# Two fused transformer layers in fp32: indexer weights moving instead of stationary, latents turned in blocks, unit and mix transfers rescheduled

## The chip, the cores and the metric

One NeuronCore of a Trainium2 chip runs the whole program. The metric is device time in microseconds (us); three runs of the kernel before are shown, and one more execution was profiled.

## What is computed

x is 256 tokens of 2048 features, fp32. Two layers follow one another.

Layer 1: h = rmsnorm(x), z = h @ w_in (2048 x 5200). The columns of z are: a pooling input, q, k, v (8 heads of 128), 16 index queries of 64, one index key of 64 and 16 index weights (the last 80 columns: "kw"). The index scores select 64 keys for each query; attention runs over them; the outputs of attention and of a pooling mixer go through w_out; then a gated feed-forward with a convolution over three tokens (w_up, w_down).

Layer 2, cut to what the change touches:

```
q_a, k_a, v_a, c_q, c_kv, k_r, gates = split(rmsnorm(h) @ w_in_2)
y_a = moba_attention(rope(q_a), rope(k_a), v_a)
qh  = rmsnorm(c_q)  @ w_uq_2          # c_q: 256 x 512, "cq"
kv  = rmsnorm(c_kv) @ w_ukv_2         # c_kv: 256 x 256, "ckv"
y_b = mla_attention(qh, kv, rope(k_r))
mixed = sigmoid(g_a) * (y_a @ w_branch_a_2) + sigmoid(g_b) * (y_b @ w_branch_b_2)
h = h + mixed @ w_out_2
h = h + (silu(hn @ w_gate_2) * (hn @ w_up_2)) @ w_down_2     # hn = rmsnorm(h)
```

## The kernel before, in words

**Products.** Every fp32 operand is split in two fp32r halves, hi and lo, and a product is hi*hi + hi*lo + lo*hi. Weights arrive in chunks of 256 rows (two k-tiles) by 512 columns into w_raw, a ring of 4 slots. ScalarE copies a chunk to w_hi (`split`, L1081), VectorE subtracts to w_lo (L1447), and TensorE (`columns`, L747 to L757) runs 2 k-tiles x 2 token tiles x 3 products = 12 matmuls with a 128x128 block of the activation stationary and 512 weight columns moving. The matmuls of one group (512 output columns) add up in one of two pairs of PSUM banks, acc[0] and acc[1].

**Order.** `plan` (L55) lists the groups with their first chunk and puts every other step at a chunk number n, in the table `at`. TensorE runs the steps of n behind chunk n. ScalarE and VectorE run them behind their split of chunk n + 3 (LEAD). SP runs them behind the load of chunk n + 7 (L513, `chunk.now - RING - LEAD - 1`); a load of chunk c waits until w_lo of chunk c - 4 is done. Each engine works through its list in order, so a step that waits holds up the splits or loads behind it. In a group whose last chunk is b - 1, the steps "at b" are the ones that follow it.

**kw.** The group of 80 columns (L128) has two chunks of eight k-tiles. `kw_columns` (L791) holds the 80 weight columns stationary and moves the 256 tokens: 16 k-tiles x 3 = 48 matmuls, the result being 80 x 256, turned. ScalarE copies it to stage (`on_copy_kw`, L1133), TensorE turns it back (`turn_kw`, L852, two transposes), VectorE scales it (`on_evac_kw`, L1453). `turn_ki` (L861) turns the doubled index key.

**Turning by blocks.** A tile is turned in two parts: VectorE transposes 32x32 blocks (L1601, L1621), then 16 SBUF-to-SBUF transfers of 32 partitions each put the blocks in their places (`move_block`, L378, its dma_start is L382; `move_unit`, L544; `move_p`, L413, whose dma_start is L419). A "unit" is one of the 12 groups of index queries, q, k, qa, ka, qn, qr that are turned so. All 16 transfers of a unit are on SP, in four steps of four. For p (attention weights) the first eight are on SP and the last eight on ScalarE's queue (`move_p_rest`). The latents cq and ckv are turned by TensorE instead (`on_turn_lat`, L986: 8 and 4 transposes of 128x128 against ident, L745), and split from PSUM by ScalarE and VectorE (`on_split_lat`, L1231, L1586).

**Mixed groups.** For n = 0 to 3 there is a group of w_branch_a_2 and one of w_branch_b_2, four chunks each. Behind the second, at b, VectorE forms the mixed columns (`on_mix_b`, L1695: two multiplications at L1699, two additions at L1702, two block transposes at L1601) and signals mix_blocks. Then 16 transfers (stage to halves) follow: for n < 3 all on SP, four each at b, b+1, b+2, b+3; for n = 3 ten on SP at b and six on ScalarE at b+1 (`move_mix_rest`). ScalarE (`on_split_mix`, L1236, L1239) waits for all 16 and makes the hi half of m_hl, VectorE (L1591, L1595) the lo half, at b+7, for n = 3 at b+3. b of one n is 8 chunks before b of the next. w_out_2 starts at b of n = 3; its chunks 4, 5, 6 and 7 wait for the lo halves of n = 2 and n = 3, two quarters each (L1048 on, `need`).

Of the kernel before, what the change touches and what calls it, by code (L numbers as in the profile page):

```python
# [6 lines left out]
F32 = mybir.dt.float32  # L7
F32R = mybir.dt.float32r
I32 = mybir.dt.int32
ALU = mybir.AluOpType  # L10
# [44 lines left out]
def plan():  # L55
# [15 lines left out]
    def copy_out(n, kind, *dest):  # L71
# [20 lines left out]
        for b in range(4):  # L92
            put(n + lead + later + b, "move", u, g, b)
# [35 lines left out]
    put(b, "copy_kw", len(groups) - 1); put(b + 1, "turn_kw", len(groups) - 1); put(b + 1, "evac_kw")  # L129
    put(b + 3, "turn_ki"); put(b + 4, "copy_ki")  # L130
# [60 lines left out]
    for n in range(4):  # L191
# [42 lines left out]
def two_layer_kernel(nc, a, out):  # L234
# [6 lines left out]
    with ctx:  # L241
# [107 lines left out]
        kw_turned, kw_scaled = sem("kw_turned"), sem("kw_scaled")  # L349
# [15 lines left out]
        p_blocks, p_moved = sem("p_blocks"), sem("p_moved")  # L365
        mix_blocks, mix_moved = sem("mix_blocks"), sem("mix_moved")
# [23 lines left out]

        def shares(part):

            return range(SP_SHARE) if part is None else range(4 * part, 4 * part + 4)
# [52 lines left out]
        def unit_there(u):  # L446

            return unit_moved[u % 4], 256 * (u // 4 + 1)

# [33 lines left out]
        def _(sp):  # L483
# [12 lines left out]
            def load(name, col, width, c):  # L496
# [15 lines left out]
                if not chunk.per:  # L512
                    if 20 <= chunk.now < 25:  # L513
                        load_constant(chunk.now - 20)
                    for step_, *args in at.get(chunk.now - RING - LEAD - 1, []):
                        if step_ == "move_x":
                            move_x(sp, args[0], shares(args[1]))
                        elif step_ == "move_mix":
                            move_mix(sp, args[0], shares(args[1]))
# [4 lines left out]
                        elif step_ == "move":  # L524
                            move_unit(*args)
# [18 lines left out]
            def move_unit(u, g, b):  # L544

                if b == 0:
                    sp.wait_ge(unit_blocks, u + 1)
                    if units[u][0:2] == ("qa", 1):
                        sp.wait_ge(scores_full, 6)
                    elif units[u][0:2] == ("ka", 1):  # L550
                        sp.wait_ge(*unit_there(u - 2))
                to, from_ = unit_target(u, g), unit_source(u)
                for a_ in range(4):
                    if units[u][0] in ("k1", "ka"):
# [1364 lines left out]
```

## Time and profile before

| | |
|---|---|
| median of three runs | 2373.63 us |
| lowest, highest | 2372.42, 2373.67 us |
| the profiled execution | 2370.55 us, span 2368.8 us from first to last instruction |
| instructions | 29833, of them 10552 matmuls |
| mean granted TensorE clock | 0.999 |
| weights and other reads from HBM | 448.12 MB, 190 GB/s over the span |

Busy time overlaps between engines. A matmul's own duration (390 ns for 512 columns) is longer than the distance between two matmuls, because they are pipelined: costs on TensorE are read from the starts. "PEld" is the load of the stationary operand, which runs beside the matmul before it. "SPq" and "ACTq" are the issues of transfers by SP and ScalarE.

### The profile page before, as it was taken

The numbers are of one execution on the slowest core, as the hardware profiler recorded it, in microseconds if no ns is written. First come the engines' busy times: TensorE is split into PE (matmuls) and PEld (weight loads), VectorE is DVE, ScalarE is ACT, GpSimd is POOL, SyncE is SP. The second block draws the span as 40 slices with busy tenths as digits, with TensorE's granted clock in tenths as the row PEclk, the third lists the DMA queues.
The fourth block names the chain that finished last, engine by engine and source line by source line (L and its number), as shares of the span: only waits on it lengthen the run. The fifth ranks groups of instructions, "written<-read, shape, count | busy, mean of one in ns | idle before, by whom it ended". The sixth has DMA issues, their size and how long they took to land.

```text
span 2368.8 us, 29833 instructions
## 1 busy us (share of the span) xinstructions
PE 2354.6 (99%) x10552; PEld 1949.5 (82%) x10552; DVE 1399.9 (59%) x1586; ACT 1186.1 (50%) x1465; POOL 59.4 (3%) x94
## 2 busy tenths in 40 slices
PE   9999999999999999999999999999999999999998
PEld 7788888888888888888888888878888888888887
DVE  6786465676776765555565554766555555554544
ACT  6445455666666544445455554544544444444443
POOL 0000000000000000001130000000000000000000
PEclk9999999999999999999999999999999999999999
DMA  9776477788787766666787666666777777767664
GB/s 304 195 216 192 153 225 209 215 227 220 202 226 219 206 219 201 201 203 195 210 215 209 181 175 197 200 202 208 230 204 200 209 203 204 209 199 220 194 195 153
DMA packets 490442, 488.24 MB, mean 206 GB/s; under 512 B 248304, under 2 KB 275568, under 8 KB 490224
## 3 DMA queue, kind: packets, MB, share of 16 engines
q1 hardware_dynamic: 467888, 482.85, 69.5%
q10 hardware_dynamic: 22464, 4.20, 0.9%
q8 instruction: 56, 0.92, 0.2%
q14 instruction: 34, 0.28, 0.0%
HBM read 448.12 MB, written 2.10 MB: 190 GB/s over the span
## 4 chain that ended last, share of the span: by engine, by line
PE 96%; SPq 1%; DVE 1%; DMA 1%; ACT 0%; issue 0%; POOLq 0%; POOL 0%; DVEq 0%; ACTq 0%
PE acc L754 31%; PE acc L756 31%; PE acc L755 31%; SPq L382 1%; PE pair_banks L923 1%; DMA w_raw<-in_w_branch_a 1%; DVE w_lo L1447 0%; PE bank L942 0%; ACT w_hi L1081 0%; DMA w_raw<-in_w_in 0%; PE pair_banks L972 0%; PE pair_banks L895 0%; PE acc L780 0%; PE acc L784 0%; PE acc L787 0%
## 5 line engine op out<-in xcount | busy, mean ns | idle before, releaser
L1447 DVE TENSOR_TENSOR w_lo<-w_raw,w_hi 128x1024 fp32r<-128x1024 f32 (+1 forms) x842 | 1024.1, 1220 | 934.8 <-ACT w_hi L1081 933.2
L1081 ACT ACTIVATE w_hi<-w_raw 128x1024 fp32r<-128x1024 f32 (+1 forms) x842 | 886.0, 1055 | 1077.1 <-PE acc L756 980.9
L754 PE MATMUL acc<-w_hi,xT 128*128 128x512 f32 (+1 forms) x2208 | 861.4, 390 | 0.0
L756 PE MATMUL acc<-w_hi,xT 128*128 128x512 f32 (+1 forms) x2208 | 856.8, 388 | 0.0
L755 PE MATMUL acc<-w_lo,xT 128*128 128x512 f32 (+1 forms) x2208 | 856.7, 388 | 0.0
L754 PEld LDWEIGHTS acc<-w_hi,xT 128*128 128x128 f32 x2208 | 414.5, 188 | 87.1 <-issue 2.7
L756 PEld LDWEIGHTS acc<-w_hi,xT 128*128 128x128 f32 x2208 | 414.5, 188 | 85.4
L755 PEld LDWEIGHTS acc<-w_lo,xT 128*128 128x128 f32 x2208 | 414.6, 188 | 83.8
L754 PE MATMUL acc<-w_hi,f_hi 128*128 128x512 f32 x688 | 267.6, 389 | 0.0
L755 PE MATMUL acc<-w_lo,f_hi 128*128 128x512 f32 x688 | 267.6, 389 | 0.0
L756 PE MATMUL acc<-w_hi,f_lo 128*128 128x512 f32 x688 | 267.6, 389 | 0.0
L755 PEld LDWEIGHTS acc<-w_lo,f_hi 128*128 128x128 f32 x688 | 129.2, 188 | 27.0
L754 PEld LDWEIGHTS acc<-w_hi,f_hi 128*128 128x128 f32 x688 | 129.2, 188 | 26.7
L756 PEld LDWEIGHTS acc<-w_hi,f_lo 128*128 128x128 f32 x688 | 129.2, 188 | 26.7
L754 PE MATMUL acc<-w_hi,y_hi 128*128 128x512 f32 x256 | 100.0, 391 | 0.0
L756 PE MATMUL acc<-w_hi,y_lo 128*128 128x512 f32 x256 | 99.6, 389 | 0.0
L755 PE MATMUL acc<-w_lo,y_hi 128*128 128x512 f32 x256 | 99.6, 389 | 0.0
L755 PEld LDWEIGHTS acc<-w_lo,y_hi 128*128 128x128 f32 x256 | 48.1, 188 | 10.0
L754 PEld LDWEIGHTS acc<-w_hi,y_hi 128*128 128x128 f32 x256 | 48.1, 188 | 9.9
L756 PEld LDWEIGHTS acc<-w_hi,y_lo 128*128 128x128 f32 x256 | 48.1, 188 | 9.9
L754 PE MATMUL acc<-w_hi,m_hl 128*128 128x512 f32 x128 | 49.9, 390 | 3.8 <-DVE w_lo L1447 3.8
L755 PE MATMUL acc<-w_lo,m_hl 128*128 128x512 f32 x128 | 49.8, 389 | 0.0
(211 smaller groups left out, 1217.4 us busy)
## 6 DMA issues: line engine op xcount, KB each, us to landing
w_raw<-in_w_up SPq DMA_DIRECT2D x264, 512.0 KB, 4.2
w_raw<-in_w_in SPq DMA_DIRECT2D x198, 512.0 KB, 4.3
w_raw<-in_w_down SPq DMA_DIRECT2D x176, 512.0 KB, 4.5
w_raw<-in_w_gate SPq DMA_DIRECT2D x88, 512.0 KB, 3.7
w_raw<-in_w_out SPq DMA_DIRECT2D x64, 512.0 KB, 4.3
w_raw<-in_w_branch_a SPq DMA_DIRECT2D x16, 512.0 KB, 4.5
w_raw<-in_w_branch_b SPq DMA_DIRECT2D x16, 512.0 KB, 4.4
halves<-stage SPq DMA_DIRECT2D x234, 32.0 KB, 2.7
```

Of the source, the lines that this page charges most:

```text
L382: return queue.dma_start(dst, src)
L754: pe.matmul(o, l, w_hi[:, slot, k, 0:width], start=start, stop=False)
L755: pe.matmul(o, l, w_lo[:, slot, k, 0:width], start=False, stop=False)
L756: last = pe.matmul(o, m, w_hi[:, slot, k, 0:width], start=False, stop=stop)
L923: last = pe.matmul(pair_banks[:, j, blk * P:blk * P + nk], q[:, blk * P:(blk + 1) * P], k[:, 0:nk], start=alone or blk == 0, stop=alone, s ...
L1081: act.activation(in_slot(w_hi, slot, width), in_slot(w_raw, slot, width), ACT.Copy).then_inc(w_split_hi, 1)
L1447: dve.tensor_tensor(in_slot(w_lo, slot, width), in_slot(w_raw, slot, width), in_slot(w_hi, slot, width).bitcast(F32), ALU.subtract).then_i ...
```

## The change

Half of every unit's transfers (blocks 2 and 3) are issued by ScalarE, in steps of their own. The kw group holds the tokens stationary (128x128) and moves the 80 weight columns, hi and lo; the result has the tokens on partitions, and VectorE scales it from acc; the two TensorE transposes and ScalarE's copies go. The transfers of mixed groups 0 to 2 come in three steps of 6, 6 and 4 at b+2 to b+4 instead of four at b to b+3; those of group 3 at b+2 on both queues (before b and b+1) and its split at b+5 (before b+3). The latents are turned by VectorE in blocks, with 16 transfers each on SP at b+2 to b+5, and are split at b+13 (before b+2). The diff, cut to its core:

```diff
         for b in range(4):
-            put(n + lead + later + b, "move", u, g, b)
+            put(n + lead + later + b, "move" if b < 2 else "move_rest", u, g, b)
         if name in ("k1", "ka"):
...
-    put(b, "copy_kw", len(groups) - 1); put(b + 1, "turn_kw", len(groups) - 1); put(b + 1, "evac_kw")
-    put(b + 3, "turn_ki"); put(b + 4, "copy_ki")
+    put(b, "evac_kw", len(groups) - 1)
+    put(b + 2, "turn_ki", len(groups) - 1); put(b + 3, "copy_ki")
...
-    put(b + 1, "turn_lat", "cq", len(groups) - 1)
-    put(b + 2, "split_lat", "cq"); put(b + 2, "lat_rstd", "cq")
+    put(b + 1, "lat_blocks", "cq", len(groups) - 1)
+    for part in range(4):
+        put(b + 2 + part, "move_lat", "cq", part)
+    put(b + 13, "split_lat", "cq"); put(b + 2, "lat_rstd", "cq")
...
-    put(b + 1, "turn_lat", "ckv", len(groups) - 1)
-    put(b + 2, "split_lat", "ckv"); put(b + 2, "lat_rstd", "ckv"); put(b + 1, "rope", "kr", len(groups) - 1)
+    put(b + 1, "lat_blocks", "ckv", len(groups) - 1)
+    for part in range(4):
+        put(b + 2 + part, "move_lat", "ckv", part)
+    put(b + 13, "split_lat", "ckv"); put(b + 2, "lat_rstd", "ckv"); put(b + 1, "rope", "kr", len(groups) - 1)
...
-        for part in range(4) if n < 3 else (None,):
-            put(b + (part or 0), "move_mix", n, part)
+        for part in range(3) if n < 3 else (None,):
+            put(b + 2 + (part or 0), "move_mix", n, part)
         if n == 3:
-            put(b + 1, "move_mix_rest", n)
-        put(b + (7 if n < 3 else 3), "split_mix", n)
+            put(b + 2, "move_mix_rest", n)
+        put(b + (7 if n < 3 else 5), "split_mix", n)
...
+        def thirds(part):
+
+            return range(SP_SHARE) if part is None else range(6 * part, min(6 * part + 6, 16))
...
+        def latents(kind):
+
+            if kind == "cq":
+                return 0, 4, over_y[0][:], over_y[4][:], cqT, G_CQ
+            return 1, 2, over_y[1][:, 0:CW], over_y[1][:, CW:2 * CW], ckvT, G_CKV
+
+        def turned_latent(kind, q):
+
+            _, nq, _, moved, _, _ = latents(kind)
+            return moved.rearrange("p (n q k) -> p n q k", n=2 * 4, q=nq)[:, :, q]
 
         def p_source(which, pair):
 
...
         def unit_there(u):
 
             return unit_moved[u % 4], 256 * (u // 4 + 1)
+
+        def move_unit(queue, u, g, b):
+
+            if b % 2 == 0:
+                queue.wait_ge(unit_blocks, u + 1)
+                if units[u][0:2] == ("qa", 1):
+                    queue.wait_ge(scores_full, 6)
+                elif units[u][0:2] == ("ka", 1):
+                    queue.wait_ge(*unit_there(u - 2))
+            to, from_ = unit_target(u, g), unit_source(u)
+            for a_ in range(4):
+                if units[u][0] in ("k1", "ka"):
+                    move = move_block(queue, to, from_, b, a_)
+                else:
+                    move = queue.dma_start(to[32 * b:32 * (b + 1)].rearrange("p (n a k) -> p n a k", n=8, a=4)[:, :, a_],
+                                        from_[32 * a_:32 * (a_ + 1)].rearrange("p (n b k) -> p n b k", n=8, b=4)[:, :, b])
+                move.then_inc(unit_moved[u % 4], 16)
...
-                            move_mix(sp, args[0], shares(args[1]))
+                            move_mix(sp, args[0], thirds(args[1]))
+                        elif step_ == "move_lat":
+                            move_lat(*args)
...
+            def move_lat(kind, b):
+
+                k, _, blocks_, moved, _, _ = latents(kind)
+                sp.wait_ge(lat_blocks, k + 1)
                 for a_ in range(4):
-                    if units[u][0] in ("k1", "ka"):
-                        move = move_block(sp, to, from_, b, a_)
-                    else:
-                        move = sp.dma_start(to[32 * b:32 * (b + 1)].rearrange("p (n a k) -> p n a k", n=8, a=4)[:, :, a_],
-                                            from_[32 * a_:32 * (a_ + 1)].rearrange("p (n b k) -> p n b k", n=8, b=4)[:, :, b])
-                    move.then_inc(unit_moved[u % 4], 16)
+                    move_block(sp, moved, blocks_, b, a_).then_inc(lat_moved[k], 16)
...
-                    h, l, o = hi[:, k * KW:(k + 1) * KW], lo[:, k * KW:(k + 1) * KW], acc[g][0][0:KW, 0:S]
-                    pe.matmul(o, h, xT_hi[:, kt], start=kt == 0, stop=False)
-                    pe.matmul(o, h, xT_lo[:, kt], start=False, stop=False)
-                    last = pe.matmul(o, l, xT_hi[:, kt], start=False, stop=kt == KT - 1)
+                    h, l = hi[:, k * KW:(k + 1) * KW], lo[:, k * KW:(k + 1) * KW]
+                    for t in range(NT):
+                        o, rows = acc[g][t][:, 0:KW], slice(t * P, (t + 1) * P)
+                        pe.matmul(o, xT_hi[:, kt, rows], h, start=kt == 0, stop=False)
+                        pe.matmul(o, xT_hi[:, kt, rows], l, start=False, stop=False)
+                        last = pe.matmul(o, xT_lo[:, kt, rows], h, start=False, stop=kt == KT - 1)
...
-            def turn_kw(g):
-
+            def turn_ki(g):
                 wait_bank(0)
                 pe.wait_ge(acc_taken[g % 2], 2 * (g // 2 + 1))
-                for t in range(NT):
-                    last = turn(0, t * KW, stage[0:KW, g % 2, 0, t * P:(t + 1) * P], KW)
-                last.then_inc(kw_turned, 1)
-                free[0] = (kw_scaled, NT)
-
-            def turn_ki():
...
-            def on_turn_stage(g, banks, wait):
-                pe.wait_ge(*wait)
-                for b in banks:
-                    wait_bank(b)
-                    four(b, lambda cc, t: stage[:, g % 2, t, (2 * b + cc) * P:(2 * b + cc + 1) * P], split_full, 1)
-                    splits.now += 1
-                    free[b] = (split_lo, splits.now)
-
-            def on_turn_lat(kind, g):
-                on_turn_stage(g, range(2 if kind == "cq" else 1), (acc_taken[g % 2], 2 * (g // 2 + 1)))
-                lats.append(splits.now)
...
-                    need = {0: (split_lo, lats[0])}
+                    need = {0: (lat_low, 1)}
                 elif name == "w_ukv_2" and col == 0:
-                    need = {0: (split_lo, lats[1])}
+                    need = {0: (lat_low, 2)}
...
-            def on_copy_kw(g):
-                finished(g)
-                stage_free(g)
-                for t in range(NT):
-                    act.activation(stage[0:KW, g % 2, 0, t * P:(t + 1) * P], acc[g % 2][0][0:KW, t * P:(t + 1) * P],
-                                   ACT.Copy).then_inc(acc_taken[g % 2], 1)
...
+            def on_move_rest(u, g, b):
+                move_unit(act, u, g, b)
...
-                o, gain = (cqT, G_CQ) if kind == "cq" else (ckvT, G_CKV)
-                for b in range(2 if kind == "cq" else 1):
-                    high([o[:, 0, 2 * b], o[:, 0, 2 * b + 1]], b, gain + 2 * b)
+                k, nq, _, _, o, gain = latents(kind)
+                act.wait_ge(lat_moved[k], 256)
+                for q in range(nq):
+                    last = act.activation(o[:, 0, q].rearrange("p (n k) -> p n k", n=2 * 4), turned_latent(kind, q), ACT.Copy,
+                                          scale=cols[:, gain + q:gain + q + 1])
+                last.then_inc(lat_high, 1)
...
-            def on_evac_kw():
-
-                dve.wait_ge(kw_turned, 1)
+            def on_evac_kw(g):
+
+                finished(g)
                 dve.wait_ge(rstd_ready, 1)
                 for t in range(NT):
-                    r, key = rstd[:, t:t + 1], T[0][:, t * KW:t * KW + IDX_DIM]
-                    dve.tensor_scalar(widx[:, t], T[0][:, t * KW + IDX_DIM:(t + 1) * KW], r, 2.0 ** -5, ALU.mult, ALU.mult)
+                    r, key = rstd[:, t:t + 1], acc[g % 2][t][:, 0:IDX_DIM]
+                    dve.tensor_scalar(widx[:, t], acc[g % 2][t][:, IDX_DIM:KW], r, 2.0 ** -5, ALU.mult, ALU.mult)
                     dve.tensor_scalar(kdup[:, t, 0:64], key, r, None, ALU.mult)
-                    dve.tensor_scalar(kdup[:, t, 64:128], key, r, None, ALU.mult).then_inc(kw_scaled, 1)
+                    dve.tensor_scalar(kdup[:, t, 64:128], key, r, None, ALU.mult).then_inc(acc_taken[g % 2], 1)
 
             def on_headsq(name, g):
...
+            def on_lat_blocks(kind, g):
+                _, nq, blocks_, _, _, _ = latents(kind)
+                dve.wait_ge(acc_taken[g % 2], 2 * (g // 2 + 1))
+                for t in range(NT):
+                    last = dve.transpose(blocks_.rearrange("p (t b q k) -> p t q b k", t=NT, b=4, q=nq)[:, t],
+                                         stage[:, g % 2, t, 0:nq * P])
+                last.then_inc(lat_blocks, 1)
+
             def on_split_lat(kind):
-                o, gain = (cqT, G_CQ) if kind == "cq" else (ckvT, G_CKV)
-                for b in range(2 if kind == "cq" else 1):
-                    low([o[:, 1, 2 * b], o[:, 1, 2 * b + 1]], [o[:, 0, 2 * b], o[:, 0, 2 * b + 1]], b, gain + 2 * b)
+                k, nq, _, _, o, gain = latents(kind)
+                dve.wait_ge(lat_high, k + 1)
+                for q in range(nq):
+                    lo_, hi_ = (o[:, n, q].rearrange("p (n k) -> p n k", n=2 * 4) for n in (1, 0))
+                    last = dve.scalar_tensor_tensor(lo_, turned_latent(kind, q), cols[:, gain + q:gain + q + 1],
+                                                    hi_.bitcast(F32), ALU.mult, ALU.subtract)
+                last.then_inc(lat_low, 1)
```

## Rows read from the trace of the kernel before

**Rows 1.** The page, busy time of each engine: us, share of the span, instructions.
```profile
PE 2354.6 (99%) x10552; PEld 1949.5 (82%) x10552; DVE 1399.9 (59%) x1586; ACT 1186.1 (50%) x1465; POOL 59.4 (3%) x94
```

**Rows 2.** Waits: engine, line, waited for; us in total, times, longest.
```profile
ACT w_hi L1081 <- PE acc L756: 980.9, 658, 8.1
...
PE acc L754 <- DVE w_lo L1447: 3.8, 2, 2.5
```

**Rows 3.** Timeline of TensorE in w_out_2: start us, us, what, [idle before].
```profile
1551.69 0.39 PE L754 MATMUL acc<-w_hi,m_hl 128*128 128x512 f32 x1
...
1562.35 0.39 PE L756 MATMUL acc<-w_hi,m_hl 128*128 128x512 f32 x1
...
1564.02 0.47 PE L754 MATMUL acc<-w_hi,m_hl 128*128 128x512 f32 x1 [1.29 <-DVE w_lo L1447]
...
1569.50 0.47 PE L754 MATMUL acc<-w_hi,m_hl 128*128 128x512 f32 x1 [2.48 <-DVE w_lo L1447]
```

**Rows 4.** The kw group: window (busy us, instructions by engine, clock, DMA) and timeline.
```profile
50.40:55.98 5.58, 5.58 (x49) 5.58 (x48) 2.66 (x3) 3.28 (x4) 0.00 (x0) 1.00 0.89 251
...
50.40 0.15 PEld L799 LDWEIGHTS acc<-xT,w_hi 128*80 128x80 f32 x1
...
50.52 0.28 PE L799 MATMUL acc<-xT,w_hi 128*80 128x256 f32 x1
```

**Rows 5.** Timeline of the weight loads behind the kw transposes.
```profile
61.54 0.19 PEld L754 LDWEIGHTS acc<-w_hi,xT 128*128 128x128 f32 x1
...
61.65 0.19 PEld L755 LDWEIGHTS acc<-w_lo,xT 128*128 128x128 f32 x1
```

**Rows 6.** Timeline of TensorE around the kw and the cq transposes.
```profile
61.23 0.39 PE L756 MATMUL acc<-w_hi,xT 128*128 128x512 f32 x1
...
61.56 0.48 PE L754 MATMUL acc<-w_hi,xT 128*128 128x512 f32 x1
...
61.88 0.40 PE L755 MATMUL acc<-w_lo,xT 128*128 128x512 f32 x1
...
1092.40 0.31 PE L754 MATMUL acc<-w_hi,xT 128*128 128x320 f32 x1
...
1092.69 0.31 PE L756 MATMUL acc<-w_hi,xT 128*128 128x320 f32 x1
...
1093.86 0.31 PE L755 MATMUL acc<-w_lo,xT 128*128 128x320 f32 x1
```

**Rows 7.** Timeline of ScalarE and its queue, transfers of p.
```profile
1210.29 1.06 ACT L1081 ACTIVATE w_hi<-w_raw 128x1024 fp32r<-128x1024 f32 x1 [1.92 <-DMA w_raw<-in_w_in]
...
1210.30 2.62 ACTq L419 DMA_DIRECT2D halves<-over_y  x4
```

**Rows 8.** Timeline of VectorE in the mixing stage, first and last group.
```profile
1491.55 1.30 DVE L1601 STREAM_TRANSPOSE stage<-stage 128x512 f32<-128x512 f32 x2
...
1492.78 2.32 DVE L1447 TENSOR_TENSOR w_lo<-w_raw,w_hi 128x1024 fp32r<-128x1024 f32 x2
...
1558.82 1.28 DVE L1699 TENSOR_TENSOR gate<-acc,gate 128x512 f32<-128x512 f32 x2
...
1561.46 1.30 DVE L1601 STREAM_TRANSPOSE stage<-stage 128x512 f32<-128x512 f32 x2
```

**Rows 9.** Timeline of SP, ScalarE and VectorE around w_out_2's first group.
```profile
1552.25 7.05 SPq L510 DMA_DIRECT2D w_raw<-in_w_out  x5
...
1556.59 1.06 ACT L1081 ACTIVATE w_hi<-w_raw 128x1024 fp32r<-128x1024 f32 x1 [0.61 <-DMA w_raw<-in_w_out]
...
1562.80 4.13 ACTq L382 DMA_DIRECT2D halves<-stage  x6
...
1570.46 1.34 ACT L1239 ACTIVATE m_hl<-halves 128x256 fp32r<-128x256 f32 x4 [1.42 <-DMA halves<-stage]
...
1570.91 1.43 DVE L1595 TENSOR_TENSOR m_hl<-halves,m_hl 128x256 fp32r<-128x256 f32 x4 [0.42 <-ACT m_hl L1239]
```

**Rows 10.** Transfers of L382 (move_block), 1480 to 1575: from issue to landing.
```profile
DMA to landing us min/median/max: 1.8/2.4/3.8
```

More of the change, by code:

```diff
@@ L348, in two_layer_kernel @@
         fgain_loaded, stored = sem("fgain_loaded"), sem("stored")
-        kw_turned, kw_scaled = sem("kw_turned"), sem("kw_scaled")
         gqk_ready, angles, tables = sem("gqk_ready"), sem("angles"), sem("tables")
@@ L365, in two_layer_kernel @@
         p_blocks, p_moved = sem("p_blocks"), sem("p_moved")
+        lat_blocks, lat_high, lat_low = sem("lat_blocks"), sem("lat_high"), sem("lat_low")
+        lat_moved = [sem("cq_moved"), sem("ckv_moved")]
         mix_blocks, mix_moved = sem("mix_blocks"), sem("mix_moved")
@@ L524, in load @@
                         elif step_ == "move":
-                            move_unit(*args)
+                            move_unit(sp, *args)
                         elif step_ == "move_p":
@@ L542, in load_constant @@
                                  allow_slow_non_contiguous=True).then_inc(const_loaded, 16)
[L544 to L552, printed above, removed]
-                for a_ in range(4):
-                    if units[u][0] in ("k1", "ka"):
-                        move = move_block(sp, to, from_, b, a_)
-                    else:
-                        move = sp.dma_start(to[32 * b:32 * (b + 1)].rearrange("p (n a k) -> p n a k", n=8, a=4)[:, :, a_],
-                                            from_[32 * a_:32 * (a_ + 1)].rearrange("p (n b k) -> p n b k", n=8, b=4)[:, :, b])
-                    move.then_inc(unit_moved[u % 4], 16)
+            def move_lat(kind, b):
+                k, _, blocks_, moved, _, _ = latents(kind)
+                sp.wait_ge(lat_blocks, k + 1)
+                for a_ in range(4):
+                    move_block(sp, moved, blocks_, b, a_).then_inc(lat_moved[k], 16)
             def pair(j, wa, ca, wb, cb):
@@ L731, in _ @@
             chunk, group, splits, copies = Count(), Count(), Count(), Count()
-            rels, atts, pvs, lats = Count(), Count(), [0], []
+            rels, atts, pvs = Count(), Count(), [0]
             roped_n, turned_any = [0], []
@@ L849, in stream @@
                 group.now += 1
-            def turn_kw(g):
+            def turn_ki(g):
                 wait_bank(0)
                 pe.wait_ge(acc_taken[g % 2], 2 * (g // 2 + 1))
-                for t in range(NT):
-                    last = turn(0, t * KW, stage[0:KW, g % 2, 0, t * P:(t + 1) * P], KW)
-                last.then_inc(kw_turned, 1)
-                free[0] = (kw_scaled, NT)
-            def turn_ki():
-                wait_bank(0)
                 turn(0, 0, kdup[:, 0])
@@ L1004, in on_turn_kn @@
                 free[0] = (copy_done, copies.now)
-            mine = {"turn_kw": turn_kw, "turn_ki": turn_ki, "turn_copy": turn_copy, "rel": on_rel, "scores": on_scores,
+            mine = {"turn_ki": turn_ki, "turn_copy": turn_copy, "rel": on_rel, "scores": on_scores,
                     "pv": on_pv, "pool_d": on_pool_d, "pool_y": on_pool_y,
-                    "turn_lat": on_turn_lat,
                     "turn_kr": on_turn_kr, "turn_kn": on_turn_kn}
@@ L1280, in on_sigmoid @@
                 act.activation(v, v, ACT.Sigmoid).then_inc(gates_open, 1)
-            mine = {"evac": on_evac, "copy_kw": on_copy_kw, "copy_ki": on_copy_ki, "copy2": on_copy2, "copy_k": on_copy_k, "relu": on_relu, "exp": on_exp,
-                    "copy_d": on_copy_d, "move_p_rest": on_move_p_rest, "copy_kr": on_copy_kr, "copy_kn": on_copy_kn,
+            mine = {"evac": on_evac, "copy_ki": on_copy_ki, "copy2": on_copy2, "copy_k": on_copy_k, "relu": on_relu, "exp": on_exp,
+                    "copy_d": on_copy_d, "move_p_rest": on_move_p_rest, "move_rest": on_move_rest, "copy_kr": on_copy_kr, "copy_kn": on_copy_kn,
                     "split_y": on_split_y, "split_x": on_split_x, "move_x_rest": on_move_x_rest, "move_mix_rest": on_move_mix_rest, "split_pool": on_split_pool,
@@ L1709, in _ @@
                     "select": on_select, "mask": on_mask, "norm": on_norm, "split_y": on_split_y, "split_x": on_split_x,
-                    "split_pool": on_split_pool, "split_lat": on_split_lat, "split_mix": on_split_mix, "res": on_res,
+                    "split_pool": on_split_pool, "lat_blocks": on_lat_blocks, "split_lat": on_split_lat, "split_mix": on_split_mix, "res": on_res,
                     "rstd": on_rstd, "lat_rstd": on_lat_rstd, "mix_a": on_mix_a, "mix_b": on_mix_b,
```

## The prediction

> **What bounds the kernel now.** I read the page's busy times first: TensorE is busy for 2354.6 of 2368.8 us, VectorE 59%, ScalarE 50% [rows 1]. Then its waits: in the whole middle of the run it waits 3.8 us, all for w_lo, in two pieces [rows 2]. Both lie in the first group of w_out_2, the product of the mixed halves [rows 3]. So time can come only from work taken off TensorE and from that one stall; every other engine matters as far as it makes a new stall. ScalarE's w_hi waits 980.9 us for TensorE to free a slot [rows 2]: the split normally runs as far ahead as the ring lets it, three chunks of 12 x 0.227 = 2.72 us (pitch: 47 steps from 1551.69 to 1562.35, [rows 3]). Of these 8.2 us a split needs 1.06 + 1.23 us, so ScalarE can be about 5.9 us late before TensorE sees it.
>
> **The indexer's 80 columns.** Now 48 matmuls have the weights (80 columns) stationary and 256 columns of xT moving; they fill the window 50.40 to 55.98, 5.6 us, 0.117 us each [rows 4]. After it there are 96, with xT (128 columns) stationary and 80 moving. No row has a moving operand so narrow with fp32r. From below, the array's time by columns: from 256 to 512 moving columns the pitch grows from 0.117 to 0.227 us, 0.43 ns a column, so 80 columns would take 0.117 - 176 x 0.00043 = 0.041 us: 96 x 0.041 = 3.9 us, a gain of 1.7. From above, if the narrow form is taken like plain fp32, the transposes of 128 columns have a pitch of 0.109 us (8 in 0.87 us), and two instructions for each product would give 192 x 0.109 = 20.9 us, +15.3. Between them lies the load of the stationary operand. A load of 80 columns lasts 0.15 us and one of 128 lasts 0.19 [rows 4, 5]: 48 columns more cost 40 ns, 0.83 ns each, so 128 columns stream for about 0.107 us. It can be seen bare where a short transpose stands before it: the load of L754 starts at 61.54 and the next at 61.65, 0.11 us, and that matmul lasts 0.48 instead of 0.39 because it waits [rows 5, 6]. Today 512 moving columns hide it; 80 don't. I take 0.11 us, the row that is nearest in kind: 96 x 0.11 = 10.6 us, **+5.0 us**. The same two loads of one xT block behind one another are not merged: L754 and L755 share their stationary operand today and each has its load.
>
> The Trainium skill, page "TensorE: Matmul & The Clock Gate", speaks on both sides. Its section "Back-to-back issue gap" gives an isolated matmul columns / 2.4 + 2.5 ns, 36 ns for 80: by that alone the group would take 3.4 us, a gain of 2.2. Its section "LDWEIGHTS (loading the stationary operand)" gives columns / 1.2, 107 ns for 128: by that 10.2 us, a loss of 4.7; the trace's 0.11 us speaks for the second.
>
> **Transposes that leave TensorE.** cq: from the start of the matmul before the eight transposes to the second one behind them 1092.69 to 1093.86, less two pitches of 0.147 (1092.40 to 1092.69 are two) = 0.87 us. ckv has four, half: 0.44. kw: 61.23 to 61.88, less 2 x 0.227 = 0.20 [rows 6]. Sum **-1.5 us**. In their place stand two block transposes on VectorE (1.3 us, as L1601) in the place of nothing, 16 transfers for each latent on SP, and the same splits, now 13 chunks behind. w_uq_2 follows cq's group by four groups, w_ukv_2 later still: cost 0. In ckv's group a chunk takes only 12 x 0.147 = 1.8 us, while SP with four transfers and a load needs 3.2, so three loads come up to 4.3 us late; the lead of 5.9 covers that. The kw group's steps lose two ScalarE copies and VectorE reads acc directly: 0, as nobody waits.
>
> **Half of the unit transfers on ScalarE.** 12 units, two steps each of four transfers. Such a step exists, for p: four take 2.6 us on ScalarE's queue and are issued while the w_hi before them runs, both from 1210.3 [rows 7]. Split and step together so take about one chunk of 2.72, and each step costs up to 0.2 us of lead, against 5.9. The densest place is qn, qr and qa beside exp and the transfers of p: two such steps, an exp and an output split within three chunks, some 3 us late. SP gets 96 issues less, but its lateness cost nothing. Both 0; if the lead were gone, each step would cost 2.6 us. The added wait for unit_blocks stands two chunks behind VectorE's step; behind it on ScalarE is the next w_hi, and behind that w_lo and TensorE, so it would cost only with VectorE over two chunks late. SP's wait for lat_blocks holds the weight loads in the same way, and comes a load later than VectorE's step: 0.
>
> **The mixed groups.** Call B(n) the moment when VectorE has turned group n. The first is 1491.55 + 1.30 = 1492.85, the last 1562.76 [rows 8]: three turns of 23.3 us, where TensorE needs only 21.8. So the chain is late by a loop of its own. From B: 16 transfers and three loads on SP until the load of w_out_2's fourth chunk is issued at 1552.25 (13.1), 4.3 to land, w_hi 1.1, w_lo 1.2, the mixing step 1558.82 to 1562.76 (3.9) [rows 8, 9]. The change sends two loads ahead of the transfers, which relieves this, but another branch takes over: ScalarE's split_mix stands before the split of that fourth chunk and waits for all 16 transfers. From B: two w_lo 2.3 [rows 8], load 0.6, 6 transfers 3.8, load 0.6, 6 transfers 3.8, load 0.6, three more pitches 1.9: 13.7; landing 2.4 [rows 10], split_mix 1.3, w_hi 1.1, w_lo 1.2, mixing step 3.9: 23.7 us. The same sum for before gives 22.6 where it measured 23.3, so 23.7 to 24.4. B(3) = 1492.85 + 71.1 = 1563.9, up to 1566.0.
>
> For n = 3 the step itself moves. Now SP and ScalarE start at B; the last transfer is there at 1570.46 and two quarters of w_lo of m_hl are done at about 1571.65, B + 8.9 [rows 9]. TensorE needs them at w_out_2's seventh chunk. After it SP stands behind two loads, which wait for two w_lo: 2.3 + 0.6, nine pitches 5.8, 1.9 to land, 1.2: B + 11.8 = 1575.7 to 1577.8. Without a stall that chunk would start at 1551.69 + 6 x 2.72 = 1568.0; it now starts at 1572.3, a loss of 4.3 in all (waits and exposed loads, [rows 3]). After: 7.7 to 9.8. ScalarE's own six, which now cost TensorE 2.48 us because they hold up a split for 8.1 us [rows 2, 9], no longer matter. Difference +3.4 to +5.5; I take **+4.5 us**. From below: if the loop is gone, B(3) is 1551.7 + 1.1 + 1.2 + 3.9 = 1557.9 and the loss 1.7, a gain of 2.6; at most all 4.3 come back.
>
> **Sum.** +5.0 - 1.5 + 4.5 = +8.0 us. The profiled execution took 2370.55 us (span 2368.8), so 2378.6 for one like it; it lies 3.1 below the median of the runs, 2373.63. For the median: **2381.6 us**.
>
> **Rivals.**
> 1. *Narrow matmuls run at their columns.* The load hides behind its neighbours (the two of one xT block could share it); kw becomes -1.7 instead of +5.0. For it: the array's time is 0.43 ns a column. Against: the bare load. Total +1.3: 2374.9. Not slower. It decides wherever the pitch is under 0.075 us. The Trainium skill's gap formula would be this rival.
> 2. *The loop of the mixed groups opens.* The loads that go first let the mixing step start on time, and the transfers land before anyone waits; the whole stall of 4.3 goes. For it: the fourth load is issued 1 to 2 us earlier. Against: split_mix and the later ten transfers. Total 5.0 - 1.5 - 4.3 = -0.8: 2372.8. Not slower.
> 3. *Both 1 and 2*: -7.5, 2366.1, faster.
> 4. *Narrow fp32r is slower than its load*, 0.15 us (as the 320-column matmul) up to two instructions of 0.109: kw +8.8 to +15.3, total +11.8 to +18.3, 2385.4 to 2391.9.
> 5. *ScalarE's lead is used up* near the exp of the second attention: one or two steps of 2.6 us behind the sum, 2384 to 2387.
>
> **How the numbers follow.** A measurement of this kernel tells 0.2% (4.7 us) from no change. Forecast 0.43 (slower), rival 1 0.16, rival 2 0.16, rival 3 0.06, rival 4 0.13, rival 5 0.06. Slower: 0.43 + 0.13 + 0.06 = 0.62, less 0.03 for a forecast whose mixed part is at its lower bound: 0.59. Faster: 0.06 plus 0.02 for rival 2 with a small kw price: 0.08. Same: 0.33. The range takes in rivals 1 and 2 and most of 4: from 2372.5 to 2388.
>
> **What would show it.** kw: 96 matmuls at a pitch of 0.11 us, a window of 10.6 us, loads back to back (0.04: rival 1; 0.15 and more: rival 4). No transposes of the latents; TensorE's wait list with w_lo or m_hl in w_out_2's fifth and seventh chunk, 8 to 9 us in all, and the last VectorE transpose at about 1566 plus what kw cost before it. ScalarE waiting for halves <- stage in each split_mix shows the new branch; if it doesn't wait, rival 2 is near. If TensorE waits anywhere between 1160 and 1260, rival 5 is at work. The forecast is wrong if the pitch is under 0.075 us or if the mixed groups lose under 3 us.

## The result, and the profile after

The changed kernel takes **2391.05 us** (median of 4 runs, 2388.82 to 2392.87), the kernel before 2373.31 beside it (4 runs): ratio 1.0079, 95% interval 1.0067 to 1.0092, so 17.7 us or 0.8% slower. The prediction said slower, with 2381.6 us (+8.0) and an upper end of 2388.0. The direction holds; of the size, less than half was foreseen, and the median lies 3 us above that upper end.

The profiled execution of the changed kernel took 2392.87 us (span 2391.1), that of before 2370.55 (2368.8): 22.3 us between the two traces, the one at the upper edge of its runs, the other below its. The page's first part answers to [rows 1], the wait list to [rows 2] (us in total, times, longest):

```profile
PE 2371.1 (99%) x10586; PEld 1965.8 (82%) x10586; DVE 1402.9 (59%) x1590; ACT 1185.4 (50%) x1463; POOL 59.1 (2%) x94
```
```profile
PE acc L783 <- DVE m_hl L1617: 4.9, 1, 4.9
PE acc L783 <- DVE w_lo L1457: 3.6, 3, 2.1
PE bank L965 <- DMA halves<-over_y: 2.0, 1, 2.0
...
ACT m_hl L1249 <- DMA halves<-stage: 15.1, 4, 4.3
```

TensorE waits 10.5 us in these three rows where it waited 3.8, so only some 7 of the 22.3 are waits. It is also busy for 16.5 us more, with 34 instructions more and 1.5 us of transposes less. Of that, some 3.5 us are work that was added (the narrow matmuls' 5.0 at full clock, less those transposes). The rest is work that ran slower. Where, the start times of the same matmuls in both traces tell, stage by stage:

```
stretch                                          after - before
up to the kw group                                   +0.6
kw group and the first 8 matmuls behind it          +13.0
latents (cq, ckv)                                    -1.4
one product with v, second attention (1256)          +2.4
branch groups, up to w_out_2                         +1.6
w_out_2 (first half)                                 +6.1
sum                                                  22.3
```

**The kw group.** Windows of TensorE (us, busy us, instructions, granted clock as a share of 2.4 GHz, DMA share, GB/s), then single matmuls and loads from the timelines:

```profile
50.00:54.00 4.00, 4.00 (x33) 1.00 1.00 303
54.00:58.00 4.00, 4.00 (x23) 0.55 0.95 210
58.00:62.00 4.00, 4.00 (x21) 0.50 0.73 167
62.00:66.00 4.00, 4.00 (x20) 0.50 0.57 157
66.00:70.00 4.00, 4.00 (x16) 0.50 0.00 0
70.00:74.00 4.00, 4.00 (x16) 0.81 0.53 139
```
```profile
51.22 0.28 PE L829 MATMUL acc<-w_hi,xT 128*128 128x80 f32 x1
51.33 0.28 PE L830 MATMUL acc<-w_lo,xT 128*128 128x80 f32 x1
...
55.14 0.41 PE L831 MATMUL acc<-w_hi,xT 128*128 128x80 f32 x1
55.35 0.41 PE L829 MATMUL acc<-w_hi,xT 128*128 128x80 f32 x1
...
68.15 0.77 PE L783 MATMUL acc<-w_hi,xT 128*128 128x512 f32 x1
68.72 0.63 PE L784 MATMUL acc<-w_lo,xT 128*128 128x512 f32 x1
69.15 0.63 PE L785 MATMUL acc<-w_hi,xT 128*128 128x512 f32 x1
```
```profile
51.19 0.19 PEld L829 LDWEIGHTS acc<-w_hi,xT 128*128 128x128 f32 x1
51.30 0.19 PEld L830 LDWEIGHTS acc<-w_lo,xT 128*128 128x128 f32 x1
...
55.28 0.33 PEld L829 LDWEIGHTS acc<-w_hi,xT 128*128 128x128 f32 x1
55.50 0.33 PEld L830 LDWEIGHTS acc<-w_lo,xT 128*128 128x128 f32 x1
```

For the first 3.5 us (32 of them, 50.96 to 54.50) the narrow matmuls start 0.11 us apart and so do their loads, as predicted. Then the granted clock falls from its upper level, 2.4 GHz, to its lower, 1.2 GHz, with no idle time on TensorE before it: loads and matmuls are now 0.21 us apart, and stay so until the group ends at 68.15. The group takes 17.2 us against 5.6 [rows 4]. The low clock outlives it: the next 8 wide matmuls have a pitch of 0.43 instead of 0.227 us, another 1.7 us. Less 0.2 for the two transposes that are gone, that makes the +13.0.

**w_out_2.** Timelines of SP's queue, of ScalarE and its queue, of VectorE and of TensorE around the last mixed group; they answer to [rows 3, 8, 9]:

```profile
1570.68 12.19 SPq L547 DMA_DIRECT2D w_raw<-in_w_out  x6
1582.92 6.64 SPq L387 DMA_DIRECT2D halves<-stage  x10
```
```profile
1580.27 3.88 ACTq L387 DMA_DIRECT2D halves<-stage  x6
...
1590.83 1.33 ACT L1249 ACTIVATE m_hl<-halves 128x256 fp32r<-128x256 f32 x4 [3.62 <-DMA halves<-stage]
```
```profile
1578.93 1.31 DVE L1623 STREAM_TRANSPOSE stage<-stage 128x512 f32<-128x512 f32 x2
...
1591.28 1.43 DVE L1617 TENSOR_TENSOR m_hl<-halves,m_hl 128x256 fp32r<-128x256 f32 x4 [2.43 <-ACT m_hl L1249]
```
```profile
1567.93 0.39 PE L783 MATMUL acc<-w_hi,m_hl 128*128 128x512 f32 x1
...
1581.49 0.47 PE L783 MATMUL acc<-w_hi,m_hl 128*128 128x512 f32 x1 [2.05 <-DVE w_lo L1457]
...
1592.09 0.79 PE L783 MATMUL acc<-w_hi,m_hl 128*128 128x512 f32 x1 [4.88 <-DVE m_hl L1617]
1592.68 0.63 PE L784 MATMUL acc<-w_lo,m_hl 128*128 128x512 f32 x1
...
1597.32 0.39 PE L783 MATMUL acc<-w_hi,m_hl 128*128 128x512 f32 x1
```

VectorE has turned the last group at 1580.2; SP reaches its ten transfers only at 1582.9, ScalarE's split waits for them until 1590.8, and the seventh chunk starts at 1592.09 instead of 1567.93 + 6 x 2.72 = 1584.25: 7.8 us lost, the lower end of what was predicted. But behind the wait of 4.9 us the clock is at its lower level too: 12 matmuls from 1592.09 to 1597.32 take 5.2 us instead of 2.7.

### The profile page after: what moved, and what is told of

Its sections match the earlier page's. It is cut to its first block, busy times and chain, and to the rows that moved or that the text cites. A ratio compares the mean times of both kernels' runs of the same rounds, so it can differ in the third digit from the quotient of the medians.

```text
span 2391.1 us, 29934 instructions
## 1 busy us (share of the span) xinstructions
PE 2371.1 (99%) x10586; PEld 1965.8 (82%) x10586; DVE 1402.9 (59%) x1590; ACT 1185.4 (50%) x1463; POOL 59.1 (2%) x94
## 4 chain that ended last, share of the span: by engine, by line
PE 95%; SPq 1%; DVE 1%; DMA 1%; ACT 0%; issue 0%; ACTq 0%; POOLq 0%; POOL 0%; DVEq 0%
PE acc L783 30%; PE acc L784 30%; PE acc L785 30%; SPq L387 1%; PE pair_banks L946 1%; DVE w_lo L1457 0%; DMA halves<-stage 0%; PE bank L965 0%; PE acc L809 0%; PE acc L813 0%; PE acc L816 0%; PE pair_banks L995 0%; DMA halves<-over_y 0%; PE pair_banks L918 0%; PE acc L831 0%
```

## The experiments

Fourteen experiments were run: one part of the change alone, one part undone, and the disputed costs by themselves. "At the scores" is the start of the first matmul into pair_banks from kiT (78.4 us in the trace of before): a shift there is what the kw group and its surroundings cost, free of everything later.

**1. The 80 columns alone** (kw_only):
```diff
-    put(b, "copy_kw", len(groups) - 1); put(b + 1, "turn_kw", len(groups) - 1); put(b + 1, "evac_kw")
-    put(b + 3, "turn_ki"); put(b + 4, "copy_ki")
+    put(b, "evac_kw", len(groups) - 1)
+    put(b + 2, "turn_ki", len(groups) - 1); put(b + 3, "copy_ki")
...
-                    pe.matmul(o, h, xT_hi[:, kt], start=kt == 0, stop=False)
...
+                        pe.matmul(o, xT_hi[:, kt, rows], h, start=kt == 0, stop=False)
...
```


> The kernel before with the indexer's 80 columns moving, nothing else. Theory 1 (narrow matmuls pull the granted clock down to half, inside the group and into the next one): the group starts at a pitch of 0.11 us, the clock then falls to half, and TensorE starts the first relu-scores (into pair_banks, from kiT) 12 to 14 us later than before; the whole run takes +12.5 to +13.5 us in its trace. Rival (the price is the load alone; the clock fell for some other part of the change, such as transfers): clock stays at full, pitch 0.11 us throughout, +4.8 us.

Measured: 2381.23 us against 2371.51, ratio 1.0039 (1.0025 to 1.0053), +9.7; at the scores +12.7. Its windows:
```profile
50.00:54.00 4.00, 4.00 (x35) 0.92 0.96 298
54.00:58.00 4.00, 4.00 (x21) 0.50 0.67 166
```
The clock falls here with none of the other parts present. That is theory 1 up to the scores. Its +12.5 to +13.5 for the whole run is missed, because the rest of the run gave some back: in w_out_2 TensorE waited 1.8 us instead of 3.8, and the span is 10.9 us longer, not 12.7.

**2. The other three parts, each alone** (mix_only, units_only, lat_only): the diff's lines for that part and no others.

> The kernel before with only the mixed groups' transfers and splits moved. Theory 1 (the loss is made in this stage alone, by the transfers of n = 3 standing two loads later and the turns of the mixing loop staying at 24 us): +6 us, with a wait of about 5 us on m_hl at the seventh chunk of w_out_2 and the clock at half after it. Rival (the stage was late only because the units' transfers and the kw group had changed the phase): under +3 us, no fall of the clock there.

> The kernel before with half of each unit's transfers on ScalarE's queue, nothing else. Theory 1 (in the second attention the transfers of p land late because ScalarE's queue carries the unit's, and TensorE waits at one product with v): +2 to +2.5 us, in one wait of about 2 us near 1256. Rival a: 0, and the wait in the changed kernel came from the latents' transfers or the shifted phase. Rival b: the wait is there and the branch stage adds another, +4 us.

> The kernel before with only the latents turned in blocks. Theory 1: the 12 transposes go from TensorE and nothing is late: -1.4 us (0.87 + 0.44 = 1.3 from the rows of before). Rival: the 32 transfers on SP make the loads or the unit transfers behind them late, and the time is the same as before or longer.

Measured against the same 2371.51 us: mix_only 2377.34, ratio 1.0025 (1.0015 to 1.0034), +5.8; units_only 2371.29, ratio 1.0000 (0.9991 to 1.0010); lat_only 2369.24, ratio 0.9993 (0.9983 to 1.0003), -2.3 and in the trace -1.3 between the scores of the first and of the second attention. mix_only has the wait on m_hl (5.6 us) and the low clock behind it: its shift grows by 7.3 us in the stage. The wait at a product with v isn't in units_only. With kw_only the four sum to +13.1, against +17.7 together.

**3. A wide matmul between the narrow ones** (kw_wide_between, kw_wide_sixth). In the first:
```diff
                         pe.matmul(o, xT_hi[:, kt, rows], l, start=False, stop=False)
+                        pe.matmul(T[3][:, 0:CW].rearrange("p (k s) -> p k s", k=2), xT_hi[:, kt, rows], xT_hi[:, 0:2], start=True, stop=True)
                         last = pe.matmul(o, xT_lo[:, kt, rows], h, start=False, stop=kt == KT - 1)
```
In the second the same line (with rows 0 to 127) stands once behind every six.

> As kw_only, with one matmul of 512 moving columns (its product goes to a bank that nobody reads) behind every two narrow ones and ahead of the third: 32 of them, at the 0.227 us of a wide one 7.3 us of added work. Theory 1 (the clock falls because of the run of narrow matmuls with nothing wide among them): granted clock stays at full through the group, 96 x 0.11 + 7.3 = 17.8 us for the group, +12.3 against before, none of it behind the group. Rival (the clock falls there whatever stands between them, for example by the transfers or by the change of bank): it falls as in kw_only, and the group takes 24 us or more.

> As kw_only, with one added matmul of 512 moving columns behind every six narrow ones: 16 of them, 3.6 us of added work. Theory 1a (a wide one in seven is enough to keep the granted clock at full): 96 x 0.11 + 3.6 = 14.2 us for the group, +8.4 against before, so less than kw_only's +12.7 though more is done. Theory 1b (it is too little): the clock falls as in kw_only, later in the group or at the same place, and the cost is +13 to +20.

Measured at the scores: +12.2 and **+8.2** us (forecast 12.3 and 8.4). The clock is whole in both, as these windows show, of kw_wide_between first:
```profile
54.00:56.00 2.00, 2.00 (x16) 1.00 0.83 224
...
66.00:68.00 2.00, 2.00 (x16) 1.00 0.30 49
```
```profile
54.00:58.00 4.00, 4.00 (x33) 1.00 0.81 184
58.00:62.00 4.00, 4.00 (x33) 1.00 0.78 180
```
By medians: 2383.42 (2 runs) against 2371.50, ratio 1.0053 (1.0033 to 1.0073), and 2381.76 (3 runs) against 2371.38, 1.0042 (1.0027 to 1.0057). kw_wide_sixth does 16 matmuls more than kw_only and reaches the scores 4.5 us earlier. The mean granted clock of every execution agrees with the traces: 0.995 or 0.996 in all five of kw_only, 0.998 or 0.999 in these five. The whole run did not become shorter, though: +10.4 by the median against +9.7 for kw_only, with intervals that overlap. Behind the scores kw_only's trace gives back 1.8 us in w_out_2, where that of kw_wide_sixth loses 1.0, with the lower clock behind a wait. So neither the transfers nor the change of bank makes the clock fall there; the unbroken run of narrow matmuls does. Taking the added 3.6 us off, the 96 narrow ones at full clock cost 4.6 more than before: the +5.0 of the prediction, less the transposes of kw.

**4. Two thirds of the loads** (kw_160). xT_hi meets 160 columns of w_hi in one matmul; the product xT_hi x w_lo is left out.
```diff
-                        pe.matmul(o, xT_hi[:, kt, rows], h, start=kt == 0, stop=False)
-                        pe.matmul(o, xT_hi[:, kt, rows], l, start=False, stop=False)
+                        pe.matmul(o[:, 0:2 * KW], xT_hi[:, kt, rows], hi[:, min(k, 6) * KW:(min(k, 6) + 2) * KW], start=kt == 0, stop=False)
```


> As kw_only, but xT_hi meets 160 columns of w_hi in one matmul, in the place of two of 80 against w_hi and w_lo (so the product xT_hi x w_lo is left out and the indexer's keys and weights are off): 64 matmuls, 32 of 160 and 32 of 80 columns. If the load of the stationary operand alone sets the pitch at full clock: 64 x 0.11 = 7.0 us for the group, +1.4 against before. Theory 1a (the clock falls with narrow matmuls also when a third fewer of them are there): the group starts at 0.11 us and the clock falls within it or right behind it, +4 to +7. Theory 1b (the wider moving operands hold the clock): +1.4 and no fall.

Measured at the scores: **+1.0 us** (forecast +1.4), and no fall:
```profile
54.00:56.00 2.00, 2.00 (x20) 1.00 0.84 189
56.00:58.00 2.00, 2.00 (x16) 1.00 0.85 194
```
```profile
56.70 0.32 PE L825 MATMUL acc<-w_hi,xT 128*128 128x160 f32 x1
56.86 0.23 PE L826 MATMUL acc<-w_hi,xT 128*128 128x80 f32 x1
56.92 0.32 PE L825 MATMUL acc<-w_hi,xT 128*128 128x160 f32 x1
57.08 0.24 PE L826 MATMUL acc<-w_hi,xT 128*128 128x80 f32 x1
57.15 0.48 PE L779 MATMUL acc<-w_hi,xT 128*128 128x512 f32 x1
```
A pair of 160 and 80 columns takes 0.22 us, like a pair of 80 and 80: the number of loads sets the time, not the columns. Whole run: 2371.12 against 2371.50 us, ratio 0.9999 (0.9989 to 1.0009), with a mean granted clock of 0.998 to 1.000 in all eight executions. Whether the wider operand keeps the clock up or the shorter group does (7.1 us here; in after_again, below, the fall came 6.2 us into the group, in the other two traces 3.2 and 3.5), no run tells apart. A kernel that held w_hi and w_lo of kw side by side could do the full product this way; that wasn't tried, and by this run it would gain nothing over before.

**5. The mixed groups in two halves** (mix_last_only, mix_first_three). Only n = 3, or only n < 3, of the change (the second with the transfers in 6, 6 and 4 as in the change):
```diff
-            put(b + (part or 0), "move_mix", n, part)
+            put(b + (2 if part is None else part), "move_mix", n, part)
         if n == 3:
-            put(b + 1, "move_mix_rest", n)
-        put(b + (7 if n < 3 else 3), "split_mix", n)
+            put(b + 2, "move_mix_rest", n)
+        put(b + (7 if n < 3 else 5), "split_mix", n)
```
```diff
-        for part in range(4) if n < 3 else (None,):
-            put(b + (part or 0), "move_mix", n, part)
+        for part in range(3) if n < 3 else (None,):
+            put(b + (0 if part is None else 2 + part), "move_mix", n, part)
```


> The kernel before with only the last mixed group (n = 3) changed: its transfers two chunks later on SP and one on ScalarE, its split two chunks later. A queue model of the stage made from the rows of both kernels gives a stall of 4.6 us at w_out_2's seventh chunk where before has 1.7 at the sixth: +3 us. Rival (the last group's shift is what costs all of mix_only's +6, and the clock falls behind the wait): +5.5 to +6. Rival (nothing, all comes from the first three): 0.

> The kernel before with only the first three mixed groups changed: their 16 transfers from the third chunk on, in 6, 6 and 4. The same model gives stalls of 0.3, 1.9 and 2.5 us, on w_lo, at branch b of the last group and at the fifth and sixth chunk of w_out_2: +3 us. Rival (these shifts are hidden: the turns of the mixing loop do not decide): 0, +/- 1. Rival (the loop opens because two loads go first): -2 to -4.

Measured against 2371.50 us: 2375.61 (nine of ten runs), ratio 1.0016 (1.0006 to 1.0026), and 2374.77, ratio 1.0015 (1.0005 to 1.0024). In the traces the stage costs +4.8 and +4.0; both together (mix_only) +7.3. The tenth run of mix_last_only took 3726.66 us at a mean granted clock of 0.596, where the nine others had 0.997 to 0.999; nothing on record says why, and it is left out. By the traces both parts cost more than the +3 that was expected of each. For the last group the wait was 6.0 us instead of 4.6; for the first three the waits in w_out_2 came as expected (2.0 and 2.5), the one in the branch stage was 1.15 instead of 0.3; and the low clock was in neither sum. Single waits of TensorE, mix_last_only first:
```profile
1563.48 0.47 PE L780 MATMUL acc<-w_hi,m_hl 128*128 128x512 f32 x1 [0.45 <-DVE w_lo L1476]
1575.21 0.80 PE L780 MATMUL acc<-w_hi,m_hl 128*128 128x512 f32 x1 [6.02 <-DVE m_hl L1632]
```
```profile
1566.83 0.47 PE L780 MATMUL acc<-w_hi,m_hl 128*128 128x512 f32 x1 [2.01 <-DVE w_lo L1476]
1572.29 0.77 PE L780 MATMUL acc<-w_hi,m_hl 128*128 128x512 f32 x1 [2.48 <-DVE w_lo L1476]
```
A first matmul that lasts 0.77 or 0.80 us instead of 0.47 runs at the lower clock: 10 matmuls of the first kernel and 7 of the second have a pitch of about 0.43 us then, 2.0 and 1.4 us on top of their waits. The halves do not add up (8.8 against 7.3). A likely reason, not tested, is that lateness which the first three have already caused hides part of the last one's wait.

**6. The changed kernel without its kw part, and once more whole** (all_but_kw, after_again):

> The changed kernel with the indexer's 80 columns as before (stationary), all other parts of the change in. Theory 1 (the kw group costs its 9 to 13 us by itself, whatever else is in): +5 to +8.5 against before. Theory 2 (the parts add up as they ran alone: mixed groups +5.8, latents -2.3, units 0): +3.5 us, and no wait at a product with v. Theory 3 (latents' and units' transfers together make the 2.0 us wait for halves at the product with v near 1256): that wait is there, and the run is 2 to 3 us over the sum of its parts.

> The changed kernel once more, to see which of its stalls come in every execution. Theory 1: kw +12.7 to +13.1, latents -1.4, w_out_2 +6 in every trace, median +16 to +19; the wait at the product with v near 1256 (2.0 us) and the one in the branch stage (1.3 us) come again. Theory 2: those two are chance of one execution and are away in this trace, which then ends 3 to 4 us earlier against before.

Measured against 2371.92 us: all_but_kw 2378.37, ratio 1.0025 (1.0016 to 1.0035), +6.5: within theory 1's bounds; the remaining 10.9 of the 17.3 are kw's. Theory 2, the plain sum of the parts, is 3.0 us short. The trace shows what is there beyond a sum, though not why: 0.7 at the product with v, 1.8 in the branch groups where mix_only had 0.9, and in w_out_2 the lower clock twice, behind a wait of 2.0 us as well as behind the one of 4.0. after_again 2389.23, ratio 1.0078 (1.0062 to 1.0093). Its trace has no wait at the product with v, but m_hl (5.6) and the branch wait (0.9) are there again, and the clock in the kw group falls 2.2 us later:
```profile
50.00:54.00 4.00, 4.00 (x36) 1.00 1.07 311
54.00:58.00 4.00, 4.00 (x32) 0.83 0.82 195
58.00:62.00 4.00, 4.00 (x21) 0.50 0.92 219
```
so +11.4 at the scores instead of 13.6. The same program, another moment of the fall: at the scores the shift is 11.4 us in one trace and 13.6 in the other.

**7. A shorter mixing loop** (mix_shared, mix_shared_lat, mix_late_lat). The first three groups share their transfers as the last does (SP's ten in 4, 4 and 2); the second adds the latents in blocks, the third moves ScalarE's six:
```diff
-        for part in range(4) if n < 3 else (None,):
+        for part in range(3) if n < 3 else (None,):
             put(b + (part or 0), "move_mix", n, part)
-        if n == 3:
-            put(b + 1, "move_mix_rest", n)
+        put(b + 1, "move_mix_rest", n)
```
```diff
-        put(b + 1, "move_mix_rest", n)
+        for part in range(2) if n < 3 else (None,):
+            put(b + (1 if part is None else 2 + part), "move_mix_rest", n, part)
```


> The kernel before with the 16 transfers of each of the first three mixed groups shared as the last one's already are: 10 on SP, in 4, 4 and 2 from the chunk where they start before, 6 on ScalarE one chunk later. The queue model made from the rows gives no stall in w_out_2 in the place of 1.7 to 4.3: theory 1: the turns of the mixing loop fall from 23.3 to 21.8 us and the run is 3 to 4.3 us faster. Rival (ScalarE's six transfers hold up a split for 4 us in each branch group and give the loss back there): 0, with waits on w_lo in the branch stage.

> mix_shared with the latents turned in blocks as in the change. Both gains add up: 3 to 4.3 and 1.3, so -4.3 to -5.6 us, ratio 0.9976 to 0.9982. Rival (the earlier phase only makes another load late): -2 or less.

> mix_shared_lat with ScalarE's six transfers of the first three mixed groups two and three chunks after the group, in threes, so that ScalarE no longer waits for VectorE's mixing step with a split behind it. Theory (that wait, ScalarE 4 us idle and 4 us issuing, made the new stalls of 2.7 and 1.9 us in the branch stage): no wait for w_lo before the last branch group, under 1.5 us in w_out_2, in all -4 to -5.6 us, ratio 0.9976 to 0.9983. Rival (the loop's length is set by the loads' landing and the weight split, whoever issues the transfers): a turn of 22.5 us or more between the mixing steps and -2 to -3 us, as with the latents alone.

Measured: mix_shared 2371.74 against 2371.92 (1.0002, 0.9992 to 1.0011); mix_shared_lat 2369.47 against 2371.92 (0.9990, 0.9981 to 0.9999); mix_late_lat 2369.88 against 2371.38 (0.9992, 0.9982 to 1.0001). The model was wrong in all three. The first rival holds; the others come nearer than the model without fitting: -2.5 where one said -2 or less, -1.5 where the other said -2 to -3. ScalarE and TensorE in mix_shared:
```profile
1541.86 4.13 ACTq L383 DMA_DIRECT2D halves<-stage  x6
1546.09 2.96 ACT L1106 ACTIVATE w_hi<-w_raw 128x1024 fp32r<-128x1024 f32 x3 [8.74 <-issue]
```
```profile
1524.49 0.50 PE L779 MATMUL acc<-w_hi,y_hi 128*128 128x512 f32 x1 [2.68 <-DVE w_lo L1475]
...
1548.46 0.50 PE L779 MATMUL acc<-w_hi,y_hi 128*128 128x512 f32 x1 [1.89 <-DVE w_lo L1475]
...
1571.97 0.47 PE L779 MATMUL acc<-w_hi,m_hl 128*128 128x512 f32 x1 [1.43 <-DVE w_lo L1475]
```
ScalarE stands 8.7 us without a split, and what w_out_2 no longer waits (1.4 us instead of 3.8), the branch groups wait, and more. With the six later (mix_late_lat) these waits shrink to one of 0.9, but the one in w_out_2 is back at 2.5, as in lat_only. Nothing here beats the latents in blocks alone by more than the measurement tells; that part, at -2.3 us with an interval that takes in no change, and mix_shared_lat, at -2.5 with one that just doesn't, are the best of all kernels run.

## Why the prediction missed the size

- **The 80 columns, the step that failed.** The prediction put this term at 96 x 0.11 - 5.6 = +5.0. The pitch, its reason (the load) and even the price at full clock (4.6 in kw_wide_sixth, 0.2 of it transposes) are right. Wrong was that the work was priced at a clock it didn't keep: no term, no rival and no end of the range asked whether the granted clock, 1.00 in [rows 4], would stay. In the trace after, 32 of the 96 took 3.5 us and the other 64 took 13.7 (54.50 to 68.15, 0.213 each), and 8 wide ones behind them 1.7 more than at full clock. The term is +13.0 in this trace and 11.4 in the second. Rival 4 had sizes of this kind (+8.8 to +15.3), and its total of +11.8 to +18.3 takes in the measured +17.7, but by luck: its mechanism is not there, as at full clock the narrow fp32r matmuls start as closely as their loads. The Trainium skill, page "TensorE: Matmul & The Clock Gate", section "LDWEIGHTS (loading the stationary operand)", puts a load at columns / 1.2, which makes an estimate of 107 ns for 128 columns; at full clock the trace agrees (0.11), at the lower it shows 0.21. The same page's "What's actually happening" lists the lower clock for an idle engine and the upper one for a busy engine; here the lower one came with TensorE busy in every record, so the measurement decides.
- **Rival 1** (columns set the pace) is refuted twice: by 0.11 us for 80 columns, and by kw_160, where 160 cost no more.
- **Transposes that leave: right.** -1.4 in the changed kernel's trace, -1.3 in lat_only, for the 1.3 of cq and ckv.
- **Half of the unit transfers on ScalarE: right at 0.** The ratio of units_only is 1.0000. Rival 5 came once, in another form: in the first trace of the changed kernel a product with v waits for a transfer of p that landed late, 6.9 us after its issue on ScalarE's queue (before: 4.2), not for the issue itself (the line stands below this list). In all_but_kw that wait is 0.5 (5.9 us to land), in after_again nothing (4.6). What makes the transfer late in some executions stays open.
- **The mixed groups: right in mechanism, too small in the sum.** The three turns from B(0) to B(3) were forecast at 23.7 to 24.4 us each and took 24.4, 23.8 and 24.5 (VectorE's ends 1507.5, 1531.9, 1555.7, 1580.2); the seventh chunk starts at B(3) + 11.9, forecast 11.8; ScalarE waits for halves <- stage in each split_mix, 15.1 us in four, so rivals 2 and 3, in which the loop opens, are refuted; the loss is 7.8 at the seventh chunk, forecast 7.7 to 9.8. Not in the sum were the low clock behind the wait (+2.5), and that some of the lateness shows already in the branch groups (+1.6). So +4.5 became +7.7. The second missing term is the same as the first.
- **Sum.** Forecast 5.0 - 1.5 + 4.5 = 8.0. Trace: 13.0 - 1.4 + 7.7 + 2.4 + 0.6 = 22.3, where 2.4 is the stage with the wait at the product with v (2.0 us of it that wait) and 0.6 a later start of the kw group; median 17.7, and the second trace, after_again, +17.8. Without the clock (64 x 0.103 = 6.6 in the group, 1.7 behind it, 2.5 in w_out_2) the first trace would stand at +11.5.

The wait at the product with v, in TensorE's timeline:
```profile
1256.81 0.67 PE L965 MATMUL bank<-halves,va 128*128 128x256 f32 x2 [1.98 <-DMA halves<-over_y]
```

## What to carry to other kernels

Where a change replaces wide matmuls by many narrow ones, or puts a long wait before TensorE, price it at both levels of the granted clock, and price what comes behind it as well: the clock stays low into the next group. If narrow ones are needed, join them to fewer, wider ones or let wide work stand between them; here a wide matmul added behind every six made that stage 4.5 us shorter, though not the whole run. So measure the stage and the whole: what one stage gains, a later one can wait away. And a transfer that is moved to a queue with a wait in front of it moves the stall, it doesn't remove it.

## What the runs showed of the hardware

- 96 matmuls of 80 columns in a row, with no idle record, fell to 1.2 GHz in three traces of three, with starts 0.21 us apart from the 32nd, the 34th and the 59th on (kw_only, after, after_again); 96 with a wide one between, and 64 of 160 and 80 columns, stayed at 2.4 GHz. The place of the fall varied by some 3 us between executions.
- At the lower clock the load is slower too: start to start 0.21 against 0.11 us, 0.33 us long against 0.19.
- Behind waits of 4.0 to 6.0 us in w_out_2 (five traces) the next matmuls were at 1.2 GHz; behind waits of 2.5 us matmuls were in units_only, mix_first_three, kw_wide_sixth and, from the fifth on, in kw_160, and were not in before, lat_only, kw_wide_between and mix_late_lat. A wait of 2.0 us was followed by 1.2 GHz in all_but_kw, but not in after and mix_only. What tells these apart is open.
- Single traces of one program differ by 4.5 us in span (2391.1 and 2386.6), mostly by the place of that fall and by one late transfer.
